# Splitting the last product of a weight unit in two column halves, in a float32 transformer block kernel

## What is computed

```python
D_MODEL, SEQ, D_FF, D_FF_2 = 1024, 256, 2816, 2816

def swiglu(u, w_gate, w_up, w_down):
    return (jax.nn.silu(u @ w_gate) * (u @ w_up)) @ w_down
...
        u = rms_norm(h, g_ffn[layer])
        h = h + swiglu(u, w_gate[layer], w_up[layer], w_down[layer])
...
        h = rms_norm_2(stream, ffn_norm_g[l])
        up = causal_depthwise_conv(h @ ffn_up[l], ffn_dw_w[l], ffn_dw_b[l])
        a, b_ = jnp.split(up, 2, axis=-1)
        stream = stream + (jax.nn.silu(a) * b_) @ ffn_down[l]
```

## Time and profile before

| | |
|---|---|
| median of 3 runs | 1110.11 us (1110.09 to 1110.68) |
| the profiled execution | 1109.47 us, its span 1107.7 us |
| mean granted clock of TensorE | 0.991 of full |
| busy: TensorE / weight loads | 1078.0 us (97%) / 1053.5 us (95%), 8781 each |
| busy: VectorE / ScalarE / GpSimd | 755.3 (68%) / 578.0 (52%) / 220.9 us (20%) |
| read from HBM | 179.27 MB, 163 GB/s over the span |
| chain that ended last | TensorE 91%, VectorE 4%, ScalarE 3%, issue 1% |

### The profile page before, as it was taken

One profiled execution on the slowest core, in us unless ns is written; L12 is line 12 of the kernel. 1 busy time (PEld: TensorE's weight loads), 2 busy tenths in 40 slices (PEclk: granted clock), 3 DMA queues, 4 the chain that ended last, 5 costly groups with the idle time before them and its releaser, 6 DMA issues.

```text
span 1107.7 us, 22257 instructions
## 1 busy us (share of the span) xinstructions
PE 1078.0 (97%) x8781; PEld 1053.5 (95%) x8781; DVE 755.3 (68%) x1233; ACT 578.0 (52%) x852; POOL 220.9 (20%) x202
## 2 busy tenths in 40 slices
PE   7998999999999999999999999999999989999997
PEld 7997999999999999999999899998899989999997
DVE  6677575555757766656555678987986657887652
ACT  5667554444545554644444544446666355555542
POOL 1431030000222110300000277785450000000000
PEclk9999999999999999999999999999999989999999
DMA  8734266657675343566555554453334534554451
GB/s 270 212 105 153 80 193 194 197 175 220 204 223 186 129 139 100 187 193 201 161 186 191 171 153 152 140 166 114 115 123 146 181 123 152 193 188 155 158 180 39
DMA packets 187941, 181.36 MB, mean 164 GB/s; under 512 B 17951, under 2 KB 186284, under 8 KB 187867
## 3 DMA queue, kind: packets, MB, share of 16 engines
q1 hardware_dynamic: 187323, 178.23, 50.9%
q0 software_dynamic: 544, 2.10, 0.7%
HBM read 179.27 MB, written 1.05 MB: 163 GB/s over the span
## 4 chain that ended last, share of the span: by engine, by line
PE 91%; DVE 4%; ACT 3%; issue 1%; DMA 0%; DVEq 0%; SPq 0%; ACTq 0%
PE ps L555 28%; PE ps L557 27%; PE ps L556 27%; DVE w_lo L394 1%; ACT w_hi L378 1%; PE ps L1981 1%; PE ps L2165 1%; PE ps L2103 1%; PE ps L1988 1%; PE ps L2172 1%; PE ps L2001 0%; PE ps L2000 0%; PE ps L1822 0%; PE ps L2127 0%; PE ps L1785 0%
## 5 line engine op out<-in xcount | busy, mean ns | idle before, releaser
L394 DVE TENSOR_TENSOR w_lo<-raw,w_hi 128x2048 fp32r<-128x2048 f32 (+3 forms) x157 | 333.4, 2137 | 137.6 <-ACT w_hi L378 137.4
L378 ACT ACTIVATE w_hi<-raw 128x2048 fp32r<-128x2048 f32 (+3 forms) x182 | 316.1, 1753 | 35.4 <-PE ps L557 25.3
L555 PE MATMUL ps<-u_hi,w_hi 128*128 128x256 f32 x944 | 265.1, 281 | 2.8 <-DVE w_lo L2343 2.3
L556 PE MATMUL ps<-u_lo,w_hi 128*128 128x256 f32 x944 | 262.4, 278 | 0.0
L557 PE MATMUL ps<-u_hi,w_lo 128*128 128x256 f32 x944 | 262.4, 278 | 0.0
L555 PE MATMUL ps<-m_hi,w_hi 128*128 128x258 f32 (+2 forms) x792 | 231.4, 292 | 6.6 <-DVE m_lo L524 4.2
L556 PE MATMUL ps<-m_lo,w_hi 128*128 128x258 f32 (+2 forms) x792 | 226.6, 286 | 0.0
L557 PE MATMUL ps<-m_hi,w_lo 128*128 128x258 f32 (+2 forms) x792 | 226.5, 286 | 0.0
L555 PEld LDWEIGHTS ps<-u_hi,w_hi 128*128 128x128 f32 x944 | 178.7, 189 | 4.0 <-DVE w_lo L2343 2.7
L556 PEld LDWEIGHTS ps<-u_lo,w_hi 128*128 128x128 f32 x944 | 178.6, 189 | 0.2
L557 PEld LDWEIGHTS ps<-u_hi,w_lo 128*128 128x128 f32 x944 | 178.6, 189 | 0.0
(11 more groups left out here) (364 smaller groups left out, 1681.0 us busy)
## 6 DMA issues: line engine op xcount, KB each, us to landing
raw<-in_w_in SPq DMA_DIRECT2D x24, 1024.0 KB, 5.3
raw<-in_w_gate SPq DMA_DIRECT2D x22, 1024.0 KB, 5.3
raw<-in_w_up SPq DMA_DIRECT2D x22, 1024.0 KB, 5.4
raw<-in_ffn_up SPq DMA_DIRECT2D x22, 1024.0 KB, 5.1
raw<-in_w_down SPq DMA_DIRECT2D x16, 768.0 KB, 4.6
raw<-in_od_w_qkv SPq DMA_DIRECT2D x12, 1024.0 KB, 5.2
raw<-in_w_down SPq DMA_DIRECT2D x16, 640.0 KB, 4.3
raw<-in_ev_w_in SPq DMA_DIRECT2D x7, 1024.0 KB, 10.1
```

Source lines behind the costliest of these rows:

```text
L378: nc.scalar.activation(w_hi[t % RING][:, 0:n], raw[t % RAW][:, 0:n], ACT.Copy).then_inc(hi_done, 1)
L394: nc.vector.tensor_tensor(w_lo[t % RING][:, 0:n], raw[t % RAW][:, 0:n], w_hi[t % RING][:, 0:n].bitcast(F32), ALU.subtract).then_inc(lo_don ...
L555: nc.tensor.matmul(out_ap, a_h, b_h, start=start and n == 0, stop=False)
L556: nc.tensor.matmul(out_ap, a_h, b_l, start=False, stop=False)
```

## The change

`feature_tile` gets an argument `halves`. With it, the last contraction step of the tile is written out: the first two of its three products are as before, and the third, low weight by high activation, becomes two products, one for the first 128 columns of the output and one for the others (128 of 256, or 130 of 258), with the same stationary operand. `stop` is on the second alone. `two_tiles` sets it for the second tile in the three feed-forwards, on the branch without `ready`; `down_unit` sets it for the second tile of every unit. The second half is now the product that adds to `unit_done`.

```diff
     units = plan["units"]
+    HALVED = (ph_ffn0, ph_ffn1, ph_ffn2)
...
-    def feature_tile(out_ap, s, nk, n, col, xh, xl, x0=0, start=True, stop=True):
+    def feature_tile(out_ap, s, nk, n, col, xh, xl, x0=0, start=True, stop=True, halves=False):
 
         hi, lo = pw(w_hi[s], nk, n), pw(w_lo[s], nk, n)
+        if halves:
+            product(out_ap, [(hi[:, kt, col:col + P], lo[:, kt, col:col + P], xh(x0 + kt), xl(x0 + kt))
+                             for kt in range(nk - 1)], start, False)
+            kt = nk - 1
+            whole, part = hi[:, kt, col:col + P], lo[:, kt, col:col + P]
+            nc.tensor.matmul(out_ap, whole, xh(x0 + kt), start=False, stop=False)
+            nc.tensor.matmul(out_ap, whole, xl(x0 + kt), start=False, stop=False)
+            for cols in (slice(0, P), slice(P, None)):
+                mm = nc.tensor.matmul(out_ap[:, cols], part, xh(x0 + kt)[:, cols], start=False, stop=stop and cols.start > 0)
+            return mm
...
-            mm = feature_tile(outs[1], s, KT, UC, P, xh, xl)
+            mm = feature_tile(outs[1], s, KT, UC, P, xh, xl, halves=ph in HALVED)
...
-                              lambda kt: a_lo[:, kt, :], x0=k0, start=k % 4 == 0, stop=k % 4 == 3)
+                              lambda kt: a_lo[:, kt, :], x0=k0, start=k % 4 == 0, stop=k % 4 == 3, halves=t == 1)
```

## The result

The changed kernel takes **1117.33 us** (median of 4 runs, 1116.76 to 1117.68) against 1110.3 us (4 runs) before: ratio 1.0069, 95% interval 1.0053 to 1.0086. It is 7.0 us slower. The profiled execution took 1117.23 us with a span of 1115.4, 7.7 us longer than the span before. I had forecast 1119.8, 9.7 us more.

What follows compares the result with a forecast made beforehand. TensorE's product stream was taken to bound the kernel. Splits adding 3.52 + 1.64 + 5.05 us, together 10.2, less 0.5 for drains, gave +9.7 us and a forecast of 1119.8 us, range 1114.0 to 1123.0.

Steps and rivals of the forecast that it cites:

- What bounds the kernel: Whole kernel: TensorE, busy 97% of the span, feeds itself without a gap, so time added to its products reaches the end.
- 96 splits, 8877 products, two load pitches in place of one: Feed-forwards and down projections: 96 products become 192, each half at a load's pitch of 111.6 ns; together 10.2 us more.
- the 8-column rows: Trace before, from 646.39 us: 8-column products with a full stationary operand start every 111.6 ns, taken as the load's pitch.
- The sign by which to tell: Profile after: first half to second, and to the next unit, 0.11 us each; 0.06 proves rival 2, 0.22 rival 3.
- rival 2: At each split: second load skipped or covered, halves take 2 x 57 ns, no loss, 1109.6 us; chance 4%.
- The drains: At ten awaited completions after a halved product: completion comes 0.05 us later, not 0.11; a credit of about 0.5 us.
- Down units, all taken at the first projection's pitch: 48 x (223.2 - 117.9) = 5.05 us: Three down projections: 48 splits, each replacing a 117.9 ns product by two of 111.6 ns; 5.05 us more.
- rivals 1 and 2: At each split: rival 1 has the load partly hidden, 84 ns per half, 1114.5 us, chance 6%; rival 2 as above.
- rival 3: At each split: the narrow product is slow in itself, at plain float32 rate; 31.0 us more, 1141; chance 9%.
- a loss of clock: Granted clock: not made a rival, since two narrow products stand among some 47 wide ones; no size or chance given.

Runs made afterwards that it cites:

- The quarters: Feed-forward units end in four products of 64 columns, against the kernel with two of 128 there and unsplit down projections: 1128.35 us, 13.3 above it.

## Why the prediction was right, and where it was not

The time came out 2.5 us under the forecast, and that it came so near is partly luck. In the down projections the sum was some 3 us too high, while +1.57 us of clock around 650 us and +0.56 us of scatter ahead of the first split, which the sum did not have either, went the other way, and the clock of the third feed-forward took 1.1 off again.

**What bounds the kernel**: right. No wait took the added time, and TensorE's busy time grew by 7.4 us of the 7.7.

**96 splits, 8877 products, two load pitches in place of one**: right in the total. Forecast for each 0.110 us in the first two feed-forwards, found 0.11 at the split and 0.125 over the unit; forecast 0.102 in the third, found 0.10. The two feed-forwards cost 1.88 and 1.86 us against 1.76 and 1.76. The quarters gave the load's pitch as 0.112 us. This was the step with the least in the trace to stand on, and the 8-column rows carried it.

**The sign by which to tell**: wrong. I had written that the first half to the second takes 0.11 us, and that a pitch of 0.06 there proves rival 2, in which a split costs nothing. The pitch is 0.057 (184.72 to 184.77, rounded), and the split costs 0.11 all the same, because the time comes at the second product of the next unit, 0.17 behind its first. The start of a product that is shorter than its load does not show what it costs; three pitches on, the sum does (0.34 against 0.23).

**The drains**: right where it could be seen. From the first half to the product behind the wait the changed kernel has 266.35 to 266.79:

```profile
266.35 0.33 PE L572 MATMUL ps<-a_hi,w_lo 128*128 128x128 f32 x2
266.79 0.35 PE L556 MATMUL ps<-a_hi,w_hi 128*128 128x256 f32 x1
```

0.44 us against 0.38 in the earlier trace rows, 0.06 more and not 0.11: the second half's start, 0.057 us behind the first, is all that is added.

**"Down units, all taken at the first projection's pitch: 48 x (223.2 - 117.9) = 5.05 us"**: this is the term that was mis-sized. It measured -0.28 + 0.72 + 1.03 = 1.5 us. The price of the splits was there (48 x 0.113 = 5.4), but the pitch of 117.9 is not a property of these products: it is one of two patterns, and with the splits all but some 40 of the 947 slow products are in the other, an estimated 907 x 4.45 ns = 4.0 us. The two leave 1.4 us, near the 1.5 measured. The trace before had it: the last down projection runs at 113.3 behind 1064 us with the same shapes as at 117.8 ahead of it. I took a pitch from one stretch and held it fixed under a change to the very stream.

**Rivals**: the second load is neither hidden nor skipped (rivals 1 and 2), and a product of 128 or 64 columns takes no longer than its load (rival 3). The 81 ns that the Trainium skill ("TensorE: Matmul & The Clock Gate", Back-to-back issue gap) gives for a sustained stream of pairs at 128 columns do not hold for these operands: a further product costs 0.11 us at 128 columns and 0.112 at 64.

**The clock**: I had left a loss of clock out of the rivals, and the two profiles of the changed kernel show none that the splits brought. But its placement, which differs between two executions of one kernel, moved +1.6 us in one stage and about -1.1 in another, near enough to cancel.

Open: what the two patterns are inside the engine. In both, a load starts 3 to 5 ns behind the product before its own. Why the feed-forward of 258 columns shows no second pattern (120.8 ns in the mean of every undisturbed tile of the kernel before) was not studied, nor was what decides in which pattern a stop leaves the stream, nor why products of 256 columns elsewhere in the second stack come every 120 ns.

## What to carry to other kernels

A product narrower than its weight load pays for the load, so cutting one in two costs a full load's pitch: 0.11 us here, for 128 and 128 columns as for 248 and 8. Look for it over some products on, and not at the narrow product's own start. Where loads and products are nearly matched, look at the starts in the timeline and not at the durations: in this kernel the stream runs in one of two patterns 4% apart, chosen anew at every stop, and one stop decided 4 us. Two halves behind each stop made it more even for 0.11 us a piece, and were not shown to make it faster; at every unit they cost more than they return.

## What the hardware showed that I had not expected

- Two self-sustaining pitches, 113.3 and 117.8 ns, for the same products of 256 columns, kept for more than 900 products in a row and changed only at interruptions.
- The times of the kernel before differ by 10 us from run to run on one chip (1102.43 to 1112.80), and by 6 us at one mean granted clock; with a split behind each stop they differ by 2.7 us.
- A product of 128 columns with a full load starts 0.057 us behind its like, and the load's pitch is paid by the products behind it.
- In or right after the 5.2 us of 8-column products the granted clock falls to 1.2 GHz, and stays there for 3.4, 6.8 or 10.2 us in different executions, with TensorE busy throughout (25.00 of the 25 us from 640 to 665); each further 3.4 us costs that stage 1.6 us (280.23, 281.80 and 283.43 us in three profiles).
